# First stage of a gated decoder layer: nine row chunks transposed by the DMA crossbar, some statistics moved to VectorE, small tables loaded later

## The reference

```python
def rms_norm(x, g):
    xf = x.astype(jnp.float32)
    y = xf * lax.rsqrt(jnp.mean(xf * xf, axis=-1, keepdims=True) + EPS)
    return (y * g.astype(jnp.float32)).astype(x.dtype)

    h = rms_norm(x, norm_g)                        # x: 2112 rows of 1024 on each core
    z = jnp.einsum('bld,de->ble', h, w_in)         # 9 parts of 1024 columns each
    u_a, v_a, gate_a, c_b, b_b, h_b, gate_b, m_a, m_b = jnp.split(z, SPLIT_IDX, axis=-1)
    u_a = jax.nn.gelu(u_a)
    v_a = layer_norm(jax.nn.gelu(v_a), ln_v_g, ln_v_b)
    s = chunk_spatial_mix(v_a, w_s, b_s)           # mixes v inside chunks of 128 rows
    y_a = u_a * s * jax.nn.silu(gate_a)
```

## Time and profile before

| | |
|---|---|
| median of three runs | 811.86 us |
| the profiled execution | 811.91 us |
| its span on the slowest core (core 7) | 809.0 us |
| spans of the eight cores | 808.4 to 809.0 us |
| TensorE busy | 791.6 us, 98% of the span |
| VectorE, ScalarE, GpSimd busy | 442.9, 285.4, 122.6 us |

### The profile page before, as it was taken

The page is one execution under the profiler, slowest core; times in us unless marked ns, Lnnn a source line. Parts: engine busy times, 40 slices in busy tenths (PEclk is TensorE's granted clock), DMA queues, the critical chain, the costliest instruction groups (busy, mean ns, idle before and its releaser), DMA issues.

```text
span 808.8 us, 13746 instructions; the slowest of 8 cores (808.4 to 809.0 us)
## 1 busy us (share of the span) xinstructions
PE 791.6 (98%) x4376; PEld 418.4 (52%) x4376; DVE 442.9 (55%) x719; ACT 285.4 (35%) x502; POOL 122.6 (15%) x243
## 2 busy tenths in 40 slices
PE   7999999999999999999999999999999999999994
PEld 3455555555555455455555545555554554444441
DVE  4587794664755565555555323333232336777776
ACT  3686555454333233233332111111111113444443
POOL 4474300000000100101001001001000001423322
PEclk9999999999999999999999999999999999999998
DMA  9955490230200600601503506008006269766532
GB/s 184 281 149 125 79 169 10 45 51 4 51 1 1 105 1 1 105 1 18 89 1 58 107 1 103 2 1 132 3 1 105 40 112 179 180 181 169 143 112 91
DMA packets 37158, 64.52 MB, mean 80 GB/s; under 512 B 20001, under 2 KB 22433, under 8 KB 37090
## 3 DMA queue, kind: packets, MB, share of 16 engines
q0 software_dynamic: 10896, 30.97, 23.5%
q1 hardware_dynamic: 26192, 32.68, 14.3%
q10 hardware_dynamic: 2, 0.00, 0.0%
HBM read 78.60 MB, written 9.58 MB: 109 GB/s over the span
## 4 chain that ended last, share of the span: by engine, by line
PE 94%; DMA 3%; POOL 1%; ACT 1%; issue 0%; DVE 0%; DVEq 0%; POOLq 0%; SPq 0%; ACTq 0%
PE ps L143 94%; DMA MG<-x 3%; PE ps L146 1%; POOL stat L152 1%; ACT SCR L149 0%; POOL WR L172 0%; DVE YA L155 0%; ACT YA L149 0%; DVE VA L155 0%; DVEq L986 0%; DVE HT L163 0%; POOLq L986 0%; POOL MG L172 0%; SPq L172 0%; ACTq L135 0%
## 5 line engine op out<-in xcount | busy, mean ns | idle before, releaser
L143 PE MATMUL ps<-HT,WR 128*128 128x512 bf16 (+2 forms) x2560 | 469.7, 342 | 0.0
L143 PEld LDWEIGHTS ps<-HT,WR 128*128 128x128 bf16 x2560 | 248.4, 98 | 200.7 <-issue 0.4
L149 ACT ACTIVATE SCR<-ps 128x512 f32<-128x512 f32 (+2 forms) x240 | 123.8, 520 | 322.7 <-PE ps L143 261.2
L155 DVE SCALAR_TENSOR_TENSOR SCR<-SCR,ps 128x512 f32<-128x512 f32 (+2 forms) x80 | 47.6, 594 | 149.6 <-PE ps L143 149.6
L152 POOL TENSOR_TENSOR stat<-stat,cst 128x1 f32<-128x1 f32 x119 | 78.1, 657 | 159.0 <-ACT SCR L149 129.0
L152 DVE TENSOR_TENSOR SCR<-SCR,ps 128x512 f32<-128x512 f32 (+2 forms) x88 | 48.2, 547 | 46.3 <-PE ps L143 38.2
L155 DVE SCALAR_TENSOR_TENSOR SCR<-SCR,cpks 128x512 f32<-128x512 f32 (+1 forms) x80 | 51.6, 644 | 37.6 <-ACT SCR L149 28.5
L143 PE MATMUL ps<-WR,HT 128*128 128x512 bf16 (+1 forms) x272 | 62.6, 381 | 3.3 <-DVE HT L163 2.1
L172 POOL DMA_DIRECT2D WR<-wt x44 | 23.8, 541 | 271.8 <-PE ps L143 270.0
L143 PE MATMUL ps<-YA,WR 128*128 128x512 bf16 (+2 forms) x320 | 63.6, 342 | 0.0
L143 PE MATMUL ps<-VA,WR 128*128 128x512 bf16 (+2 forms) x320 | 63.6, 342 | 0.0
(11 more groups left out here) (81 smaller groups left out, 515.5 us busy)
## 6 DMA issues: line engine op xcount, KB each, us to landing
WR<-wt POOLq DMA_DIRECT2D x44, 512.0 KB, 8.3
y<-YA SPq DMA_DIRECT2D x16, 512.0 KB, 4.1
MG<-x SPq DMA_DIRECT2D x12, 512.0 KB, 6.0
WR<-x SPq DMA_DIRECT2D x8, 512.0 KB, 4.7
VA<-x SPq DMA_DIRECT2D x8, 512.0 KB, 5.5
WR<-w_v POOLq DMA_DIRECT2D x4, 512.0 KB, 12.4
MG<-x POOLq DMA_DIRECT2D x4, 512.0 KB, 14.4
HT<-w_pg POOLq DMA_DIRECT2D x2, 1024.0 KB, 9.6
```

The costliest lines, as they stand in the source:

```text
L143: return lambda e: e.matmul(out, lhsT=lhsT, rhs=rhs, start=start, stop=stop)
L149: return lambda e: e.activation(out=out, in_=in_, func=func, **kw)
L155: return lambda e: e.scalar_tensor_tensor(out=out, in0=in0, scalar=scalar, in1=in1, op0=op0, op1=op1)
```

## The change

- From chunk 8 on (XT0 = 8) A3 and A4 are left out. Their place takes A34(c): one DMA transpose, issued by SP right behind A2(c), from HTOK straight into HT. An HTOK buffer is free again when its transpose has landed.
- For chunks 11, 13 and 15 the sum of squares moves from ScalarE (A0) to one VectorE instruction (A0d), which stands at the end of iteration c - 1; GpSimd's two operations follow it as before.
- blk, ci_s, BC1 and BC2 are loaded behind the loop and no longer at i = 14.

```diff
+        def A0d(c):
+            r, sl = crow(c), c % NXI
+            S.op("dve", STT(JUNKD[0:r, :], XIN[sl][0:r, :], INVD, XIN[sl][0:r, :], ALU.mult, ALU.mult, st(c, 0, r)),
+                 reads=[B_xin[sl]], writes=[B_junkd, B_stat[c]])
+            S.op("pool", TT(st(c, 1), st(c, 0), cc(C_EPS), ALU.add), reads=[B_cst], writes=[B_stat[c]])
+            S.op("pool", TT(st(c, 2), st(c, 1), cc(C_NH), ALU.pow), reads=[B_cst], writes=[B_stat[c]])
...
+        XT0 = 8
+        B_xt = [Buf("xt0"), Buf("xt1"), Buf("xt2")]
+
+        def A34(c):
+            r, t0, hs = crow(c), c * 128, c % 3
+            S.dma("sp", [XT(HT3[:, :, t0:t0 + r], HTOK[hs][0:r, :])], B_xt[hs], reads=[B_htok[hs]], writes=[B_hT[c]])
+
+        def on_dve(c):
+            return c >= 11 and c % 2 == 1
...
             if 5 <= i - 1 < NCH:
                 A2(i - 1)
+            if XT0 <= i - 1 < NCH:
+                A34(i - 1)
             if 3 <= i - 3 < NCH:
                 Bmm(i - 3, (0, 1))
-            if 4 <= i - 2 < NCH:
+            if 4 <= i - 2 < XT0:
                 A3(i - 2)
                 A4(i - 2)
...
-            if 5 <= i + 1 < NCH:
+            if 5 <= i + 1 < NCH and not on_dve(i + 1):
                 A0(i + 1)
...
+            if 5 <= i + 1 < NCH and on_dve(i + 1):
+                A0d(i + 1)
             if NXI + 3 <= i + 5 < NCH:
                 x_load(i + 5)
...
-            if i == 14:
-                emit_blk_dmas()
-                S.dma("sp", [DMA(ci_s[:, :], ci0_d[:, :])], B_cis[0], writes=B_cis)
-                S.dma("sp", [DMA(BC1, ln_g_d.partition_broadcast(128))], B_bc1, writes=[B_bc1])
-                S.dma("sp", [DMA(BC2, ln_b_d.partition_broadcast(128))], B_bc2, writes=[B_bc2])
+        emit_blk_dmas()
+        S.dma("sp", [DMA(ci_s[:, :], ci0_d[:, :])], B_cis[0], writes=B_cis)
+        S.dma("sp", [DMA(BC1, ln_g_d.partition_broadcast(128))], B_bc1, writes=[B_bc1])
+        S.dma("sp", [DMA(BC2, ln_b_d.partition_broadcast(128))], B_bc2, writes=[B_bc2])
```

More of the change, by code:

```diff
@@ L152, in TT, with STT @@
     return lambda e: e.tensor_tensor(out=out, in0=in0, in1=in1, op=op)
-def STT(out, in0, scalar, in1, op0, op1):
-    return lambda e: e.scalar_tensor_tensor(out=out, in0=in0, scalar=scalar, in1=in1, op0=op0, op1=op1)
+def STT(out, in0, scalar, in1, op0, op1, acc=None):
+    return lambda e: e.scalar_tensor_tensor(out=out, in0=in0, scalar=scalar, in1=in1, op0=op0, op1=op1, accum_out=acc)
 def TS(out, in0, s1, s2, op0, op1=None):
@@ L255, in build_program @@
         GROW = SCR[0:1, 1024:2048]
+        JUNKD = SCR[:, 2048:2560].bitcast(BF16)
         B_xin = [Buf("xin%d" % i) for i in range(NXI)]
@@ L259, in build_program @@
         B_htok = [Buf("htok0"), Buf("htok1"), Buf("htok2")]
-        B_junk, B_junkx = Buf("junk"), Buf("junkx")
+        B_junk, B_junkx, B_junkd = Buf("junk"), Buf("junkx"), Buf("junkd")
         B_bc0h = [Buf("bc0_0"), Buf("bc0_1")]
@@ L565, in build_program @@
         for b in B_t1 + B_t2:
-            b.inherit(B_junk, B_junkx, B_gr)
+            b.inherit(B_junk, B_junkx, B_junkd, B_gr)
         homes = [(0, 1024, B_htok[2]), (2048, 4096, B_ws), (4096, 6144, B_bc1), (6144, 8192, B_bc2)]
```

## The result

The changed kernel takes 821.8 us (median of four runs, 817.7 to 823.9) against 811.9: a ratio of 1.0116 [1.0069, 1.0162]. It is slower, as forecast, but by 10 us where I forecast 3.4, and above the top of the range, 818.3.

What follows compares the result with a forecast made beforehand. TensorE, busy 98%, was taken to bound the kernel. To 811.9 us came 1.8 for transpose 11 landing late behind Bd, net of the transposes removed, and 1.6 for the clock: 815.3 us, range 809.5 to 818.3.

Steps and rivals of the forecast that it cites:

- TensorE bounds, and 3.9 us come off it: First stage: TensorE, busy 98%, loses eight transposes of 0.45 us and one of 0.33; alone this gives 808.0 us.
- A2(10) at 53.8, one step later through A0d: VectorE, iteration 10: A0d(11), priced at 1.28 us, goes ahead of A2(10), which ends at 53.8, not 52.5.
- the second rival: Bd out of the way in time, VectorE sets the pace at 4.0 us a chunk: 811.3 us, chance 0.27.
- Transpose 10, "issue 53.9, landing 57.2: one us late": SP's transpose of chunk 10, issued after A2(10), lands at 57.2 against a need at 56.2.
- Bd lands at 64.5 (59.3 to 65.1), transpose 11 0.9 behind it, at 65.4: SP's queue: Bd, slow beside a weight load, holds up transpose 11; the stage ends 1.8 us later (−3.0 to +4.8).
- The pause before Bmm(11): TensorE ends Bmm(10) at 60.7 and idles 4.7 us until transpose 11 lands.
- The 9.3 us row is nearer to waiting than to turns: Bd's earlier 9.3 us landing read as waiting for the weight load; with turns, transpose 11 would come some us earlier.
- Chunks 12 to 16 then come in time: After Bmm(11), transposes 12 to 16 land at about 66 to 81 against needs from 68.9 to 83.
- break-even of 63.6: Start of Bmm(11) at which the change neither gains nor loses: 61.5 before, plus 2.1 us of transposes still to come.
- The clock, 1.6 us: TensorE's pause before Bmm(11) lowers its clock to half speed for a while, costing nothing to 3.4 us; 1.6 taken.
- The tables cost nothing behind the loop: blk, ci_s, BC1, BC2 land by about 100, before BC1 is wanted at 106.39: no cost, six us of cover.
- The range: Total time from 809.5, half outside the all-hidden case, to 818.3, which is 811.9 + 4.8 + 1.6.

Runs made afterwards that it cites:

- both hindrances away: The changed kernel with Bd issued at i = 17 and the weight loads at i = 5, 18, 19, 20: ratio 0.9965 against the kernel before, −2.8 us.
- the fillers: Twelve useless matmuls put before Bmm(11) in the changed kernel with weight loads aside, Bd still at i = 11: 812.3 us, 0.9987 against 1.0015 without them.
- the kernel with extra transposes: The kernel before, TensorE's transposes kept, plus one unread DMA transpose per chunk from 8 on, tables behind the stage: 824.9 us, ratio 1.0139.

## Why the prediction was right or wrong

- **TensorE bounds, and 3.9 us come off it**: right. With both hindrances away the gain is 2.8 us [1.9, 3.7], with the squares back 3.5, of which 0.7 to 0.9 lies outside the span. A change inside the span is thus not carried over to the time one for one, as I had it: outside the span lie 2.9 us before and 1.9 in the changed kernel.
- **A2(10) at 53.8, one step later through A0d**: right on core 5, where transpose 10 was issued at 53.66. That VectorE then sets the pace (the second rival) shows only with both hindrances away, with 3.8 us a chunk where I had 4.0, and costs about a us.
- **Transpose 10, "issue 53.9, landing 57.2: one us late"**: this step failed. I took 3.3 us, the median of the earlier trace rows, though the weight load beside it stood in my own next paragraph. It landed at 57.3 to 62.6 on the eight cores, 4.6 to 8.9 us after its issue, and TensorE paused for 1.8 to 6.7 us before Bmm(10). The row that was nearest was not the median but the 8.6 of the same rows, which the earlier trace rows show beside a GpSimd load. I used that row for a transpose behind a slow copy, and not for one beside the load.
- **Bd lands at 64.5 (59.3 to 65.1), transpose 11 0.9 behind it, at 65.4**: the order was right on every core, transpose 11 landing 1.0 to 1.2 us behind Bd; on four cores Bd came at 62.0 to 64.8, on the other four at 66.0 to 67.7, above my bound; on three of these four the weight load itself took 9.6 to 11.1 us, with a transpose beside it, where it had taken 8.7. But Bd was only part of the cause: without it transpose 11 still landed at 62.4 to 65.5, against 63.1 to 68.7. The pause before Bmm(11), 4.7 us in the forecast (57.2 + 3.5 to 65.4), came on six cores with 1.5 to 4.3; on cores 0 and 5 Bmm(10) ended too late for it to show.
- **"The 9.3 us row is nearer to waiting than to turns"**: misread. In front of Bd on SP's queue stood x_load(16), issued at 52.58; by the row below (kernel before, issues from 52.5 to 53.8) it landed at 57.7, 3.9 us before the weight load's 61.6. If SP's copies follow one another, Bd's own part was 57.7 to 62.5, 4.8 us against the 3.5 of an undisturbed copy. This fits the Trainium skill's rule (DMA: Bandwidth & Descriptors, Queues, rings and completion order) that the engines take turns between the queues. The rule gave no reason to expect Bd several us earlier.

```profile
MG<-x SPq DMA_DIRECT2D x1, 256.0 KB, 5.1
```

- **"Chunks 12 to 16 then come in time"**: this failed too, and on core 5, which set the time, it cost the most. There Bmm(11) started at 68.91, 5.3 us behind the break-even of 63.6, where the forecast had 1.8 and 1.6 of clock; the pause before Bmm(12) then added 5.0 us and 2.3 of clock, where the forecast had nothing. On cores 3 and 6 this pause was 1.1 and 1.2 us, on the other five there was none over 0.3. I asked only when their A2 end, and not what else is on the DMA engines when they are issued; the load of i = 13 is, beside transposes 12 to 14, and that of i = 16 beside transpose 16.
- **The clock, 1.6 us**: right that it falls, on all eight cores. On six of them the stretch at 0.50 lasted 3.4 us, so at most 1.7 us of work were lost, about the forecast (the fillers give 2.3, with 1.7 to either side); it was too small for the slow ones, core 4 with 6.8 us at 0.50 and core 5 with two stretches that cost 2.9 and 2.3.
- **The tables cost nothing behind the loop**: right. At their old place they cost 20 us more than the changed kernel, in one run.
- **One number for eight cores**: the forecast reckoned one core. Its +3.4 lies near the middle of the cores (+5.0), in part by luck, since the pauses stood elsewhere than forecast. The time is that of the unluckiest of eight, and collisions on the DMA engines spread the cores over 11 us.
- **The range**: its top allowed for Bd alone. No rival had a transpose that is slow for another reason than its queue; that was the case that came.

The Trainium skill says (DMA: Bandwidth & Descriptors, Rules for kernel authors) that a transpose next to ordinary DMAs needs nothing. That stands beside its warning on transposes from two queues and is about the data; on time these runs differ, 3.0 to 3.5 us alone and 4.6 to 23.5 beside loads (the longest is transpose 11 on core 5 of the kernel with extra transposes).

## What to carry to other kernels

A DMA on the path between two busy engines is priced by what else is on the DMA engines until it lands, not by the median of its line: list every load in flight then, on all queues, and take the row that was measured in such company. A load issued just behind it counts too: the weight load that delayed transpose 10 was issued 0.6 us after it. When a step is moved onto DMA, move the large loads around it first; here that, with the squares back on ScalarE and chunk 8 back on TensorE, turned +9 us into −5. And where every core runs the same program, a step whose length depends on such company is paid at the worst of eight.

## What was not expected of the hardware

- The packets of a transpose of 128 x 1024 bf16 take 1.36 us of all 16 DMA engines, those of a copy of the same bytes 0.74; alone it lands in 3.0 us.
- The harm is mutual: a weight load of 8.7 us took up to 17.4 beside transposes and Bd, and the engines, busy, moved 17 to 61 GB/s where 231 followed.
- SP is held as well: the issue of a transpose, 1.2 us on SP, took 4.4 and 6.9 on core 5 of the changed kernel while earlier ones had not landed.
- A load on ScalarE's queue, unconverted, slows a transpose about as much as one on GpSimd's: 5.6 to 9.6 us against 6.1 to 9.2.
